# Query projection of an expert layer: head 0's choice in one block, some low splits on GpSimd, new places for early expert rows

## The reference, cut to what matters

```
q = z @ peer_wq                                   # 256 x 2048, 8 heads x 2 x 128
s1, s2 = q1 @ keys1, q2 @ keys2                   # 128 scores each, per head
v1, i1 = top_k(s1, 16);  v2, i2 = top_k(s2, 16)
top_s, expert = top_k(all 256 sums v1 + v2, 16)   # 16 experts per token and head
gate = softmax(top_s)
act  = gelu(peer_u[expert] . z)                   # a row of 2048 per token, head, expert
out  = sum over heads and experts of gate * act * peer_v[expert]
```

## Time and profile before

| | us |
|---|---|
| median of 3 runs | 2511.88 (2511.83 to 2512.01) |
| span of the profiled execution | 2510.6 |
| PE busy | 2164.5 (86%) |
| DVE busy | 1507.2 (60%) |
| POOL busy | 713.0 (28%) |
| ACT busy | 698.7 (28%) |
| DMA traffic | 755.63 MB, mean 301 GB/s |

### The profile page before, as it was taken

The page is one execution under the profiler, slowest core; times in us unless marked ns, Lnnn a source line. Parts: engine busy times, 40 slices in busy tenths (PEclk is TensorE's granted clock), DMA queues, the critical chain, the costliest instruction groups (busy, mean ns, idle before and its releaser), DMA issues.

```text
span 2510.6 us, 32227 instructions
## 1 busy us (share of the span) xinstructions
PE 2164.5 (86%) x12036; PEld 1607.1 (64%) x12036; DVE 1507.2 (60%) x2142; ACT 698.7 (28%) x1163; POOL 713.0 (28%) x650
## 2 busy tenths in 40 slices
PE   8999999999999999999987668776787668776686
PEld 8999999999999999999842223332233223332232
DVE  5445655555656677857976555655565555655545
ACT  5444544554344345635220000100010000100011
POOL 3000000000001413130574444444344434444442
PEclk9999999999999999999998899888998889988998
DMA  9634444465657555474999999999999999999997
GB/s 273 200 114 153 137 154 146 134 215 172 221 168 245 157 168 166 142 229 151 382 422 422 421 421 421 422 422 422 422 422 421 421 422 422 422 421 421 422 421 299
DMA packets 281388, 755.63 MB, mean 301 GB/s; under 512 B 12032, under 2 KB 213200, under 8 KB 214608
## 3 DMA queue, kind: packets, MB, share of 16 engines
q0 software_dynamic: 74432, 539.07, 51.9%
q1 hardware_dynamic: 206624, 215.28, 27.1%
q10 hardware_dynamic: 240, 0.07, 0.0%
HBM read 752.26 MB, written 2.10 MB: 300 GB/s over the span
## 4 chain that ended last, share of the span: by engine, by line
PE 51%; DMA 35%; DVE 7%; issue 3%; POOL 3%; ACT 1%; ACTq 0%; POOLq 0%; DVEq 0%
PE PS L1755 40%; DMA RZ<-in_peer_u,idxu 18%; DMA RAW<-in_peer_u,idxu 17%; PE PS L2041 6%; DVE RZ L1601 2%; POOL EX L621 2%; DVE RAW L1601 2%; DVE WL L1097 1%; PE PS L1889 1%; DMA EX<-in_peer_v,idxv 1%; PE PS L1826 1%; PE PS L1966 1%; PE PS L1867 1%; POOL RAW L621 0%; DVE SM L1601 0%
## 5 line engine op out<-in xcount | busy, mean ns | idle before, releaser
L2041 PE MATMUL PS<-EX,RK 128*128 128x512 f32 x1968 | 910.4, 618 | 312.9 <-ACT RK L1062 185.8
L2041 PEld LDWEIGHTS PS<-EX,RK 128*128 128x128 f32 x1968 | 378.2, 197 | 844.3 <-issue 715.3
L1755 PE MATMUL PS<-XH,WH 128*128 128x256 f32 x2832 | 781.9, 285 | 2.6 <-ACT XH L753 1.5
L1755 PE MATMUL PS<-XH,WL 128*128 128x256 f32 x2832 | 775.9, 283 | 0.0
L1755 PE MATMUL PS<-XL,WH 128*128 128x256 f32 x2832 | 705.4, 283 | 0.0
L1097 DVE TENSOR_TENSOR WL<-RAW,WH 128x1024 fp32r<-128x1024 f32 x380 | 474.2, 1258 | 380.3 <-ACT WH L710 376.8
L710 ACT ACTIVATE WH<-RAW 128x1024 fp32r<-128x1024 f32 x380 | 400.1, 1059 | 543.1 <-PE PS L1755 534.0
L1755 PEld LDWEIGHTS PS<-XH,WH 128*128 128x128 f32 x2832 | 543.3, 192 | 3.9 <-issue 1.9
L1755 PEld LDWEIGHTS PS<-XH,WL 128*128 128x128 f32 x2832 | 543.3, 192 | 0.0
L1755 PEld LDWEIGHTS PS<-XL,WH 128*128 128x128 f32 x2832 | 501.2, 192 | 0.4
L1601 DVE CUSTOM_DVE_ANT_0 RZ<-RZ 128x2048 f32<-128x2048 f32 x126 | 288.8, 2292 | 250.6 <-DMA RZ<-in_peer_u,idxu 250.2
(11 more groups left out here) (342 smaller groups left out, 1330.6 us busy)
## 6 DMA issues: line engine op xcount, KB each, us to landing
RAW<-in_w_in SPq DMA_DIRECT2D x110, 1024.0 KB, 5.1
RAW<-in_w_out SPq DMA_DIRECT2D x32, 1024.0 KB, 5.6
RAW<-in_w_ple_gate SPq DMA_DIRECT2D x16, 1024.0 KB, 6.1
RAW<-in_peer_wq SPq DMA_DIRECT2D x16, 1024.0 KB, 6.0
RAW<-in_w_up_a SPq DMA_DIRECT2D x8, 1024.0 KB
RAW<-in_w_up_b SPq DMA_DIRECT2D x8, 1024.0 KB, 5.6
EX<-in_peer_v,idxv POOLq DMA_INDIRECT x252, 28.0
RZ<-in_x SPq DMA_DIRECT2D x2, 1024.0 KB, 6.9
```

What stands on the lines that cost most here:

```text
L1755: ins = mm(o[:, t, :], left, right, start=(begins and k == t == m == 0), stop=(ends and k == QUARTER_KT - 1 and m == len(pairs) - 1), skip ...
L2041: ins = mm(bank(4 * (1 - hf) + c), left, right[:, 512 * c:512 * (c + 1)], start=False, stop=True, skip_group_check=True)
```

## The change

- PE: `mean_square(1, 1)` moves ahead of the last quarter of panel 0. `key_scores(0)` moves from the middle of panel 1 into `token_order(0)`, after its first 6 of 16 products.
- ACT: the square root moves ahead of the split of the last quarter of panel 1; the scores of head 0 are copied out ahead of the square for `token_norm(0)`.
- DVE: the 11 pieces of head 0's choice run in one block after the query of panel 0. `token_norm(0)` follows the query of panel 1. Dots, and the pieces of the second choice, have new places; 16 dots lie between (2, 0) and (7, 2), panel and quarter.
- POOL: eleven low splits of `wq` (list `POOLED`) are made by POOL, three ahead of its wait for `idx_ready` and eight between gathers. They count on a semaphore of their own, `wl_pool`; PE, SP and POOL wait by `wait_low` for both counts.
- Places: `EARLY` uses three units of `RAW` and not four, later in the order; `EARLY_DOTS` has new values; two U gathers of row 1 (k = 0, 1) are issued ahead of the first V gather, after dots 13 and 14.

```diff
+POOLED = ((2, 0), (2, 1), (2, 2), (3, 1), (3, 3), (4, 1), (4, 3), (5, 1), (5, 3), (6, 1), (6, 3))
...
-        EARLY_DOTS = {4: 1, 5: 2, 6: 3, 7: 4, 9: 5, 11: 6, 12: 7, 14: 8}
-        EARLY_UNITS = {8: (6, 0), 10: (6, 1), 13: (7, 0), 15: (7, 1)}
-        RAW_DOTS = (9, 11, 14, 16)
+        EARLY = [sm_a, sm_b, z_b, qhigh, sm_a, sm_b, z_b, sm_a, sm_b, z_b, qlow, sm_a, raw_unit(6, 0), raw_unit(6, 1), sm_b, raw_unit(7, 0)]
+        EARLY_DOTS = {4: 1, 5: 2, 6: 3, 7: 5, 8: 6, 9: 7, 11: 8, 14: 9}
+        EARLY_UNITS = {12: (6, 0), 13: (6, 1), 15: (7, 0)}
+        EARLY_SCORED = 10
+        EARLY_SPLITS = {4: (3, 1), 5: (3, 3), 7: (4, 1), 8: (4, 3), 10: (5, 1), 11: (5, 3), 12: (6, 1), 13: (6, 3)}
+        RAW_DOTS = (13, 14, 16)
...
+        def wait_low(eng, j, q):
+
+            n = sum(1 for at in POOLED if at <= (j, q))
+            eng.wait_ge(S["wl_ready"], quarters_before("wq", j) + q + 1 - n)
+            if n:
+                eng.wait_ge(S["wl_pool"], n)
...
+            for q in range(3):
+                split_low(2, q)
             g.wait_ge(S["idx_ready"], 1)
             for k in range(TOPK):
+                if k in EARLY_SPLITS:
+                    split_low(*EARLY_SPLITS[k])
                 if k in EARLY_DOTS:
                     g.wait_ge(S["u_used"], EARLY_DOTS[k])
...
+            for k in range(2):
+                g.wait_ge(S["u_used"], RAW_DOTS[k])
+                gather_u(1, 1, k, reused=False)
             for k in range(V_SLOTS):
...
+            split_next("wq", 0, quarters=(0, 1, 2))
+            v.wait_ge(S["rt_ready"], 3)
+            do(v.reciprocal(rstd[:], rt[:]))
+            query(0)
+            split_next("wq", 0, quarters=(3,))
+            v.wait_ge(S["sc_evac"], 1)
+            for piece in range(11):
+                choose(0, 0, 0, piece)
...
+            second = {(4, 0): (0, 1), (5, 0): (2, 3), (5, 4): (4,), (6, 0): (5,), (6, 2): (6, 7), (6, 4): (8, 9), (7, 0): (10,)}
+            dots = {(2, 0): 1, (2, 2): 2, (2, 4): 3, (3, 0): 4, (3, 2): 5, (3, 4): 6, (4, 0): 7, (4, 2): 8, (4, 4): 9, (5, 0): 10, (5, 2): 11,
+                    (6, 0): 12, (6, 2): 13, (6, 4): 14, (7, 1): 15, (7, 2): 16}
...
-                product("wq", j, operand="z3" if j == 0 else None, middle=(lambda: key_scores(0)) if j == 1 else None,
-                        third=(lambda: key_scores(j - 1)) if 2 <= j <= SCORED else None)
+                product("wq", j, operand="z3" if j == 0 else None,
+                        third=(lambda: mean_square(1, 1)) if j == 0 else (lambda: key_scores(j - 1)) if 2 <= j <= SCORED else None)
                 if j == 0:
                     pe.wait_ge(S["keys_evac"], 4)
-                    mean_square(1, 1)
                     pe.wait_ge(S["h2_ready"], 8)
-                    token_order(0).then_inc(S["h2t_done"], 1)
+                    token_order(0, between=lambda: key_scores(0)).then_inc(S["h2t_done"], 1)
```

More of the change, by code:

```diff
@@ L133 @@
 LOOPED = (
-    "wh_ready", "wl_ready", "w_used", "qv_ready", "th_ready", "gin_ready", "oa_ready", "s_done", "s_free", "t_ready", "exp_done", "e_ready",
+    "wh_ready", "wl_ready", "wl_pool", "w_used", "qv_ready", "th_ready", "gin_ready", "oa_ready", "s_done", "s_free", "t_ready", "exp_done", "e_ready",
     "pt_done", "pts_ready", "pv_done", "o_free", "up_done", "x1_ready", "tg_looped", "pg_done", "x2_ready", "h2_ready", "sq_step",
@@ L247, in raw_unit @@
             return raw[:, 2 * ((STARTS["wq"] + j) % 2) + u].rearrange("p k n -> p (k n)")
-        EARLY = [SM[:, 0:D], SM[:, D:2 * D], znat[:, 1, :], qhigh, SM[:, 0:D], SM[:, D:2 * D], znat[:, 1, :], qlow,
-                 raw_unit(6, 0), SM[:, 0:D], raw_unit(6, 1), SM[:, D:2 * D], znat[:, 1, :], raw_unit(7, 0), qlow, raw_unit(7, 1)]
-        EARLY_DOTS = {4: 1, 5: 2, 6: 3, 7: 4, 9: 5, 11: 6, 12: 7, 14: 8}
-        EARLY_UNITS = {8: (6, 0), 10: (6, 1), 13: (7, 0), 15: (7, 1)}
-        RAW_DOTS = (9, 11, 14, 16)
+        sm_a, sm_b, z_b = SM[:, 0:D], SM[:, D:2 * D], znat[:, 1, :]
+        EARLY = [sm_a, sm_b, z_b, qhigh, sm_a, sm_b, z_b, sm_a, sm_b, z_b, qlow, sm_a, raw_unit(6, 0), raw_unit(6, 1), sm_b, raw_unit(7, 0)]
[4 more added lines that the diff above has]
+        RAW_DOTS = (13, 14, 16)
         gfbc = g2bc
@@ L408, in load @@
                     slot = 2 * (n % 2) + u
-                    if n >= 2:
+                    if section == "wq" and j >= 2:
+                        wait_low(sp, j - 2, 2 * u + 1)
+                    elif n >= 2:
                         sp.wait_ge(S["wl_ready"], quarters_before(section, j, i) + (2 * u + 2 - 2 * QUARTERS))
@@ L635, in gather_v, with split_low @@
                 gather(peer_v, vbuf[k % V_SLOTS], v_landed[k % V_SLOTS], idxv, par, k)
+            def split_low(j, q):
+                slot, at = 2 * ((STARTS["wq"] + j) % 2) + q // 2, QUARTER_KT * (q % 2)
+                g.wait_ge(S["wh_ready"], quarters_before("wq", j) + (q + 1))
+                g.tensor_tensor(WL[:, q], raw[:, slot, at:at + QUARTER_KT, :], WH[:, q].bitcast(f32), ALU.subtract).then_inc(S["wl_pool"], 1)
+            for q in range(3):
+                split_low(2, q)
             g.wait_ge(S["idx_ready"], 1)
             for k in range(TOPK):
+                if k in EARLY_SPLITS:
+                    split_low(*EARLY_SPLITS[k])
                 if k in EARLY_DOTS:
@@ L642, in _ @@
                     j, u = EARLY_UNITS[k]
-                    g.wait_ge(S["wl_ready"], quarters_before("wq", j) + 2 * u + 2)
-                if k == 7:
+                    wait_low(g, j, 2 * u + 1)
+                if k == EARLY_SCORED:
                     g.wait_ge(S["sc_done"], 4)
                 gather(peer_u, EARLY[k], u_landed[k % U_SLOTS], idxu, 0, k)
+            for k in range(2):
+                g.wait_ge(S["u_used"], RAW_DOTS[k])
+                gather_u(1, 1, k, reused=False)
             for k in range(V_SLOTS):
@@ L651, in _ @@
                 gather_v(0, 0, k, reused=False)
-            for k in range(U_AHEAD):
-                if k < 4:
+            for k in range(2, U_AHEAD):
+                if k == 2:
                     g.wait_ge(S["u_used"], RAW_DOTS[k])
@@ L1024, in _ @@
                 if j < 7:
-                    split_next("wq", j, quarters=(0, 1) if j == 1 else (0, 1, 2))
-                if 1 <= j <= SCORED:
+                    split_next("wq", j, quarters=(0, 1, 2))
+                if 2 <= j <= SCORED:
                     key_scores(j - 1)
-                if j < 7:
-                    split_next("wq", j, quarters=(2, 3) if j == 1 else (3,))
                 if j == 0:
@@ L1032, in _ @@
                     a.activation(rt[:], bank(3)[:, 0:TOK], ACT.Sqrt, scale=1.0 / D, bias=eps[:, 0:1]).then_inc(S["rt_ready"], 1)
+                if j < 7:
+                    split_next("wq", j, quarters=(3,))
+                if j == 0:
+                    key_scores(0)
                     token_norm(0)
@@ L1619, in weights, with query @@
                     .then_inc(S["w_ready"], 1)
[L1621 to L1624, removed]
+            def query(j):
+                b = bank_of("wq", j)
+                done("wq", j)
+                if j == 4:
+                    v.wait_ge(S["u_used"], 4)
+                v.tensor_tensor(qp[:, 2 * j:2 * j + 2, :], tiles2(b), rstd2, ALU.mult).then_inc(bank_free[b], 1)
@@ new lines, in _ @@
+            split_next("wq", 0, quarters=(0, 1, 2))
[6 more added lines that the diff above has]
+                choose(0, 0, 0, piece)
+            v.tensor_copy(idxu[:, 0, :], expf[:]).then_inc(S["idx_ready"], 1)
+            v.tensor_copy(idxv[:, 0, :], expf[:]).then_inc(S["idx_ready"], 1)
+            v.wait_ge(S["idx_ready"], 2)
@@ L1625, in _ @@
+            second = {(4, 0): (0, 1), (5, 0): (2, 3), (5, 4): (4,), (6, 0): (5,), (6, 2): (6, 7), (6, 4): (8, 9), (7, 0): (10,)}
+            dots = {(2, 0): 1, (2, 2): 2, (2, 4): 3, (3, 0): 4, (3, 2): 5, (3, 4): 6, (4, 0): 7, (4, 2): 8, (4, 4): 9, (5, 0): 10, (5, 2): 11,
+                    (6, 0): 12, (6, 2): 13, (6, 4): 14, (7, 1): 15, (7, 2): 16}
             dotted = 0
-            for j in range(8):
+            for j in range(1, 8):
                 for q in range(QUARTERS + 1):
-                    if j < 7 and q < QUARTERS:
+                    if j < 7 and q < QUARTERS and (j + 1, q) not in POOLED:
@@ L1629, in _ @@
                         split_next("wq", j, quarters=(q,))
                     if q == QUARTERS:
[L1631 to L1638, removed]
@@ L1640, in _ @@
-                    if (j, q) == (1, 0):
-                        token_norm(0)
[L1642 to L1649, removed]
@@ L1650, in _ @@
-                    if (j, q) == (3, 1):
+                        query(j)
+                    if (j, q) == (1, 4):
+                        token_norm(0)
+                        v.wait_ge(S["znat_ready"], 1)
+                    for k in range(dotted, dots.get((j, q), dotted)):
+                        dot(0, 0, 0, k, EARLY[k])
+                    dotted = dots.get((j, q), dotted)
```

(15 more changed lines are left out.)

## The result

The changed kernel takes **2527.32 us** (2527.00 to 2527.48) against 2511.9 us of the kernel before, timed beside it: a ratio of 1.006 with a 95% interval of 1.0048 to 1.0072, so 15.4 us slower. The profiled execution spans 2525.2 us against 2510.6, 14.6 more. The prediction had 2511.0 us, with a range of 2503 to 2517.5, and 17% for slower.

The account below looks back on a forecast made before the run. The last half was taken as a fixed, full DMA queue, so only idle DMA time before it counts. Dot 14 at 1254.8 against 1254.2 gave +0.6 us, -1.4 with less blocking; -0.9 taken: 2511.0 us, range 2503 to 2517.5.

Parts of the forecast that it names:

- dot 14 now gates the V gathers: POOL's queue: row 1's k = 0 and 1, ahead of the V gathers, wait for dots 13 and 14.
- d14 + 21.9: Gather queue: 25th landing is dot 14's end plus 4.5 us for the next gather and seven V gathers of 2.49.
- break-even of 1254.2: DVE: the end of dot 14 at which the 25th gather would land as in the kernel before.
- the end of dot 14: DVE, panel 6: 63.7 us of work from 1179.3 gives 1243.0; 11.8 us of blocking makes it 1254.8.
- The blocking: POOL's 2.4 us splits hold up DVE's two-operand instructions: 4 us in the choice, 11.8 us up to dot 14.
- The layout behind the sum: Eight POOL splits laid against DVE's instructions in order: six cost 1.0 to 2.4 us each, (4, 3) and (5, 3) nothing.
- PE's stall in panel 4: PE waits for POOL's split (4, 1) from 1202.9 to 1207.0, about 4 us; PE ends at 1255.5.
- Idle DMA ahead of row 1's k = 1: Sign to look for: a DMA idle for 2 to 3 us before the gather issued right after dot 14.
- the time changes by what the 25th landing changes: Row 1's first U rows are 25th in POOL's order, through at 1276.07 before; from 1276 both kernels carry on alike.
- The upper end of the gain: Idle DMA time around the query projection: at most 12.4 us, or about 11 us idle; 10.7 taken.
- a case near it: Rival: blocking falls beside DVE's idle time; 7 us gained, 2504.6, or 10.7 and 2501 with no blocking; 28%.
- The slower one: Rival: POOL's queue becomes the bound, 69 us of work in 76; dot 14 at 1262.2, 8 us late, 2519.9; 17%.

Follow-up runs that it names:

- e1: The first experiment: changed kernel with row 1's first two U gathers put back behind the eight V gathers; 2517.53 us, 1.0023 of the kernel before.
- e3: Changed kernel with V gathers ahead of row 1's U gathers and all eleven splits back on VectorE; 2515.49 us, 1.0013 of the kernel before.
- e5: Kernel before with only the early choice: PE's and ACT's new order, 11 pieces in one block, z's norm after panel 1; 2514.24 us, 1.0007.
- e7: e3 with the three panel 2 splits on GpSimd again, ahead of the indices; the other eight stay on VectorE; 2514.79 us.
- e8: e7 with dots spread, only 9 ahead of panel 7, and the second choice done by the end of panel 6; 2508.77 us, 0.9986 of the kernel before.
- e10: e8 with split (2, 2) back on VectorE behind the choice and dot 8 ahead of the second choice's piece 4; 2506.87 us, 0.9978 of the kernel before.
- e2: Changed kernel with all eleven splits back on VectorE, order of gathers, early choice and places kept; 2525.62 us.
- e9: e8 with the eight later splits on GpSimd again, order on VectorE and of gathers kept; 2532.05 us, 1.0081 of the kernel before.

## Why the prediction was wrong

**Wrong step: "dot 14 now gates the V gathers".** The two gathers placed ahead wait for dots 13 and 14 and also, inside `gather_u`, for `idx_ready` of row 1. I had left the last piece of the second choice out of DVE's sum and never asked who waits for it. In the kernel before nobody did at once: the indices came at about 1252 and row 1's gathers stood behind eight V gathers. My formula, d14 + 21.9, assumed further that k = 0 was through by then; both gathers came after the indices, back to back. With dot 14's measured end, 1258.5, the formula gives 1280.4 for the 25th landing; the trace has 1295.3 - 5.0 = 1290.3. Of this error of 9.9 us, 3.0 are the indices behind dot 14 and 2.5 the transfer of k = 0. The other 4.4 lie in the start on empty DMA engines: the issue of k = 0 took 2.38 us beside a dot, where I had reckoned with 0.94 for k = 1, and the DMA share was still 0.34 from 1264 to 1266. With 0.6 for the forecast 1254.8 against the break-even of 1254.2, and 3.7 for dot 14's own delay, this gives 14.2 us. That the first experiment gave back 9.8 us, nearly the same as 9.9, is a coincidence: it took away the wait for dot 14 as well, and PE's late end then held the V gathers instead.

**Mis-sized: the end of dot 14,** 1258.5 instead of 1254.8. The first gather's landing was missing: DVE waited 4.8 us ahead of dot 1, which began at 1189.63, and my sum had no wait there. The blocking came to 0.7 us more than predicted, and DVE's own work to 1.8 less; together that is the 3.7. Issued at 1180.07, the first gather landed 9.5 us later, with a unit of weights and the next three gathers in flight; no row of before showed how long a first gather takes.

**The blocking: right in sum, in part by luck.** Split alone: predicted 2.4, measured 2.40. Indices: predicted 1178.9, measured 1179.0. Two steps of the choice were blocked (2.19 and 2.44 us where 0.17 and 0.42 are usual), but the first is an instruction with one operand, which I had counted as free. After them seven dots and splits are stretched, by 12.5 us in sum, against 11.8 predicted. The layout behind the sum was not right: split (3, 1), priced at 2.4, ran while DVE waited for the first rows and cost nothing, and (4, 3) and (5, 3), priced at nothing, cost 2.2 and 1.6. This pair, a dot of DVE and POOL's split (4, 1), is typical:

```profile
1204.08 4.43 DVE L1629 CUSTOM_DVE_ANT_0 SM<-SM,RZ 128x2048 f32<-128x2048 f32 x1
```

```profile
1203.84 2.52 POOL L654 TENSOR_TENSOR WL<-RAW,WH 128x1024 fp32r<-128x1024 f32 x1
```

**Right, but not the point.** PE's stall in panel 4 was predicted as about 4 us; it stood idle 4.1 us there, in three pieces (0.15, 2.49 ahead of 1206.50, and 1.43 ahead of 1214.82). It ended at 1258.8 instead of 1255.5. One wait that the layout did not have is of 2.69 us, for a low split of DVE, and PE's granted clock then stood at 0.50, the lower of its two levels, from 1240 to 1242; a matmul took 0.41 us there and 0.28 at full clock:

```profile
1238.96 0.39 PE L1790 MATMUL PS<-XH,WH 128*128 128x256 f32 x1 [2.69 <-DVE WL L1125]
...
1239.95 0.41 PE L1790 MATMUL PS<-XH,WL 128*128 128x256 f32 x1
```

Idle DMA ahead of row 1's k = 1 was foretold as 2 to 3 us; there were more than 8. That the time changes by what the 25th landing changes held roughly: in e1, e3, e5, e7 and e8 the span came out 0.2 to 1.4 us longer than the landing of row 1's first U rows would have it, and 2.9 in e10.

**The upper end of the gain was too generous.** I took 10.7 us for what earlier indices could bring at best, and 28% for a case near it. The run with the early choice alone brought nothing, as four early gathers only move the idle time unless dots follow them, and the best kernel found brings 5.5.

**The rivals.** The slower one named the right engine and a wrong queue entry: POOL did not bind by the sum of its work, 69 us by my count, but by one entry that waited. Its price from the port, 8 us, fits no run in this order (2 us between e2 or e3 and its partner, 2.7 between e1 and e7). The remaining 5.4 us that the first experiment left come from PE's end at 1258.7. Of them, 2 to 3 are the splits on GpSimd (e3, e7), and the rest goes with the order on DVE (dots and second choice), since e8 removes it and more.

On the page that I had weighed (the Trainium skill, "SBUF — State Buffer", "Who interferes with whom"): its rule that whoever starts first holds the pair for the whole instruction is confirmed here by the pair above, where the dot that starts 0.24 us behind the split waits for its end. Its inferred remark that a `tensor_tensor` does not stall descriptor generation is not: a gather issued beside a low split of DVE took 1.76 us instead of 0.94 and ended 0.8 after it, and eight gathers issued beside dots took 2.2 to 3.0 us. DVE's low split, blocked by POOL's, and POOL's gather behind both:

```profile
1219.34 3.07 DVE L1125 TENSOR_TENSOR WL<-RAW,WH 128x1024 fp32r<-128x1024 f32 x1
```

```profile
1218.92 2.39 POOL L654 TENSOR_TENSOR WL<-RAW,WH 128x1024 fp32r<-128x1024 f32 x1
1221.47 1.76 POOL L634 DMA_INDIRECT RZ<-in_peer_u,idxu  x1 [0.16 <-issue]
```

## What to carry to other kernels

When an operation is moved ahead in an in-order queue, list every semaphore that its helper waits for, not only the one that the edit names, and ask when each comes; all that stands behind it inherits the latest. Work given to an engine whose queue also holds waiting DMAs costs what the waits ahead of it cost, whatever its own duration: the same eight splits cost 2.7 us in one order (e1 against e7) and 23 in another (e9 against e8). In front of a full DMA queue, an earlier start gains only if the transfers after the first few can follow; add up the idle DMA time up to the point from which both kernels are alike, and compare the sums, not the starts.

## What the runs showed of the hardware

- GpSimd's low split of 128x1024 with two SBUF operands takes 2.40 us alone, twice VectorE's 1.23, and shuts out VectorE's two-operand instructions meanwhile; a dot of 2.28 us became 4.43. A small `TENSOR_SCALAR` of 128x16 on VectorE was shut out too (2.19 us for 0.17).
- Plain loads took longer when more gathers were in flight: from 1176 to 1210 a 1 MB unit took a median of 19.6 us in e3 and 8.0 in the kernel before. In e3 gathers went in packets of 7.3 KB (7.34 MB in 1008), units of weights in 1.0 KB (4.83 MB in 4780). The Trainium skill ("DMA: Bandwidth & Descriptors", "SWDGE vs HWDGE vs iDMA") says that an engine takes its queues in turn, switching between packets; that would favour the larger packets and agrees with the direction, but no run here varies the packet size, so the cause stays argued.
- The first gather of the changed kernel landed 9.5 us after its issue began, against 2.49 us of transfer at 422 GB/s. The DMA share was 0.53 from 1180 to 1184 and 1.00 or more from there, and three more gathers were issued by 1185.7. How much of the 9.5 us is sharing and how much is the start, no run here separates.
